# Second mixer: the delta branch woven into eight weight chunks, with results kept in DRAM

## The chip, the core and the metric

The kernel runs on one core of one Trainium2 chip. The metric is the device time of one execution in microseconds (us); of several executions the median is taken. The engines are named as in the profile: PE multiplies matrices (PEld loads its weights), DVE is the vector engine, ACT the scalar engine, POOL is GpSimd, SP issues DMAs.

## The reference, cut to what matters

Three blocks run one after the other on 512 tokens of width 1024, all in float32. The change is in the mixer of the second block. Its input `h` is multiplied by one wide matrix whose columns feed three recurrent branches (a: gated delta rule, b and c: attention with a decay per channel), their output gates and three "shares":

```python
proj = x @ w_in
(a_q, a_k, a_v, a_beta, a_dt, a_g, b_q, b_k, b_v, b_lr, b_g,
 c_q, c_f, c_i, c_g, m_a, m_b, m_c) = split(proj)
aq, ak, av = split(silu(causal_short_conv(concat[a_q, a_k, a_v], gdn_conv)))
aq = l2_normalize(aq) * 128 ** -0.5;  ak = l2_normalize(ak)
g_a = -exp(a_log) * softplus(a_dt + dt_bias)
o_a = gated_rms_heads(gated_delta_rule(aq, ak, av, sigmoid(a_beta), g_a), a_g, gdn_norm)
o_b = gated_rms_heads(diag_decay_linear_attention(b_q, b_k, b_v, log_alpha), b_g, gla_norm)
o_c = gated_rms_heads(diag_decay_linear_attention(silu(c_q), k_c, c_i, log_f), c_g, hgrn_norm)
y = (sigmoid(m_a) * (o_a @ w_br_a) + sigmoid(m_b) * (o_b @ w_br_b)
     + sigmoid(m_c) * (o_c @ w_br_c)) @ w_out
h = layer_norm(2 ** 0.25 * h + y)
```

## The kernel before

**Projections.** A weight chunk is 512 columns (1024 x 512 values, 2 MB), loaded by SP in two halves of 1 MB into one ring (`load_ahead`), cut by DVE into a high and a low part (`split_piece`, L122 and L124), and multiplied by PE in three products for each pair of tiles (L150 to L152): 96 matmuls of 128x512 for a chunk. The plan of chunks (`plan_two`) fixes their order, and a chunk is loaded and split about one chunk ahead. The split of the first half of chunk c+1 waits until PE has used the first half of chunk c, that of the second half until chunk c is done. `project` runs chunks alone, with two groups of four PSUM banks. `project_along` runs them with a `Side`: a piece of other work whose four engine parts are written as generators, each `yield` ending a step. A table for each engine says how many steps must stand in the engine's program before each slot; on PE there are eight slots for a chunk, of 12 matmuls each, in the order of `PAIRED`, with a choice of banks. Each turn of ACT that empties a bank is such a place too, and so is each split on DVE. So the order on each engine is fixed when the program is built, and a step that waits holds up all that stands behind it on its engine.

**Stages.** `stage` is a block in which the engines meet only by semaphores, with a barrier of all engines behind it (L45, L49). The second mixer is a row of such stages:

- `delta_in`: chunks `aqkv` (three, with a convolution on DVE) and `beta_dt` (8 columns wide, two short rows).
- `unit_rows` (L1502): norms of q and k by matmuls with ones (L1533), a reciprocal and a root, the factors spread by matmuls (L1537). SP also writes the 23 zero tiles of `moe_entries` here (L1511), 12 MB, wanted only in the later mixture of experts.
- soft maximum, decay, columns, values: short stages with one or two engines at work.
- `delta_half`, twice (two heads each), three stages each: `delta_scores`, `delta_inverse` (a triangular inverse by seven levels, each with 8 and then 16 matmuls per pair of groups, L1640 and L1645/L1646, and eight DVE passes), `delta_solve` (forward substitution over four token tiles, L1658, L1663, L1691, then outputs L1669).
- `close` for the branch: `gdn_gates` projects the gate `ag` and the share `ma` (three chunks; DVE normalizes the branch output beside them), `transpose` turns it, `gdn_out` multiplies it by `w_br_a` and by the share.
- `gla_in` (chunks `bqk`, `bv` and `blr`, 16 columns), gate and decays, `channel_decay` (L1750), `close`.
- `hgrn_in` (chunks `cq`, `cf`, `ci`), `hgrn_bound` and others, `channel_decay`, `close`; then `mix_T` and `out2`.

`core.h` holds the mixer's input from start to end, since `out2` adds it; `core.x` holds u and v of the delta branch and later the sum of the branches.

Of the kernel before, what the change touches and what calls it, by code (L numbers as in the profile page):

```python
# [7 lines left out]

# [367 lines left out]
def project_along(nc, core, name, xT, runs, banks, side, kt=KD):  # L376
# [6 lines left out]
    with stage(nc, name, "freed", "loaded", *side.signals) as (block, freed, *sems):  # L383
# [45 lines left out]
        @block.scalar  # L429
        def _(act):  # L430
            pace = Pace(side.act, act, sems)
            for i, (c, j, (_, _, _, how)) in enumerate(chunks):
# [1069 lines left out]
def unit_rows(nc, core, d, qkT):  # L1502

    n = 2 * GDN_HEADS
    with buffers(nc, squares=[P, n, SEQ], pick=[P, n, n], scale_row=[n, SEQ]) as (squares, pick, scale_row), \
            stage(nc, "unit", "picks", "squared", "summed", "inverted", "rooted", "spread") as (
                block, picks, squared, summed, inverted, rooted, spread):
        @block.sync
        def _(sp):
            for s in range(ROW_TILES):  # L1510
                sp.dma_start(core.moe_entries[s * P:(s + 1) * P, :], d["const_zero_rows"]).then_inc(core.entries_cleared, 16)  # L1511

        @block.gpsimd
        def _(pool):
            nc.gpsimd.memset(pick[:], 0.0)
            pool.drain()
            for f in range(n):
                done = nc.gpsimd.memset(pick[:, f, f:f + 1], 1.0)
            done.then_inc(picks, 1)

        @block.scalar
        def _(act):
            for f in range(n):
                nc.scalar.activation(squares[:, f, :], qkT[:, f, :], ACT.Square).then_inc(squared, 1)
            act.wait_ge(inverted, 1)
            nc.scalar.activation(scale_row[:], scale_row[:], ACT.Sqrt).then_inc(rooted, 1)

        @block.tensor
        def _(pe):
            pe.wait_ge(picks, 1)  # L1530
            for f in range(n):
                pe.wait_ge(squared, f + 1)
                mm = nc.tensor.matmul(core.ps[0:n, 0, :], pick[:, f, :], squares[:, f, :], start=f == 0, stop=f == n - 1)  # L1533
            mm.then_inc(summed, 1)
            pe.wait_ge(rooted, 1)
            for f in range(n):
                nc.tensor.matmul(core.ps[:, (f + 1) % 8, :], core.ident[0:n, f:f + 1].to_broadcast([n, P]), scale_row[:],  # L1537
                                 start=True, stop=True).then_inc(spread, 1)

        @block.vector  # L1540
        def _(dve):
            dve.wait_ge(summed, 1)
            nc.vector.tensor_scalar(scale_row[:], core.ps[0:n, 0, :], 1e-6, None, ALU.add)
            dve.drain()
            nc.vector.reciprocal(scale_row[:], scale_row[:]).then_inc(inverted, 1)
            for f in range(n):
                dve.wait_ge(spread, f + 1)
                nc.vector.scalar_tensor_tensor(qkT[:, f, :], qkT[:, f, :], GDN_DK ** -0.5 if f < GDN_HEADS else 1.0,
                                               core.ps[:, (f + 1) % 8, :], ALU.mult, ALU.mult)


def delta_half(nc, core, half, qkvT, cum_rows, cols, vb, u, o, masks):


    H = GDN_HEADS
    heads = (2 * half, 2 * half + 1)
    kind_beta, kind_cum, kind_minus = 0, 1, 2
    with buffers(nc, keys=[P, 2, PACKED], attn=[P, 2, PACKED], edge=[P, NT, P], diag=[P, 8, P], rhs=[P, 2, P]) as (
            keys, attn, edge, diag, rhs):
        inv, invT = (qkvT[:, q:q + 2, :].rearrange("p q (n t) -> p (q n) t", t=P) for q in (2 * H, 2 * H + 2))  # L1560
        part, prod = (core.tmp[:, q:q + 2, :].rearrange("p q (n t) -> p (q n) t", t=P) for q in (0, 2))
        with stage(nc, f"delta_scores{half}", "spread", "edged", "decayed", "scored", "applied") as (
                block, spread, edged, decayed, scored, applied):
            @block.tensor
            def _(pe):
                for n, h in enumerate(heads):
                    if n:
                        pe.wait_ge(decayed, n)
                    nc.tensor.matmul(core.ps[:, 0, :], core.ident[0:H, h:h + 1].to_broadcast([H, P]), cum_rows, start=True, stop=True).then_inc(spread, 1)
                    for m, first in enumerate((H + h, h)):  # L1570
                        for s in range(NT):
                            if n or m:
                                pe.wait_ge(applied, NT * (2 * n + m - 1) + s + 1)
                            nc.tensor.matmul(core.ps[:, 1 + s, 0:SEQ - s * P], qkvT[:, H + h, s * P:(s + 1) * P],
                                             qkvT[:, first, s * P:], start=True, stop=True).then_inc(scored, 1)

            @block.scalar
            def _(act):
                for n, h in enumerate(heads):
                    act.wait_ge(edged, n + 1)  # L1580
                    decay_strips(nc, core, 0, edge, lambda s: cols[:, kind_minus, h, s:s + 1], attn[:, n])
                    act.drain().then_inc(decayed, 1)

            @block.vector
            def _(dve):
                for n, h in enumerate(heads):
                    dve.wait_ge(spread, n + 1)
                    if n:
                        dve.wait_ge(decayed, n)
                    nc.vector.tensor_tensor(edge[:], core.ps[:, 0, :].rearrange("p (s t) -> p s t", s=NT),  # L1590
                                            core.causal[:].unsqueeze(1).to_broadcast([P, NT, P]), ALU.add).then_inc(edged, 1)
                    dve.wait_ge(decayed, n + 1)
                    for m, dst in enumerate((keys, attn)):
                        dve.drain()
                        for s in range(NT):
                            dve.wait_ge(scored, NT * (2 * n + m) + s + 1)
                            nc.vector.tensor_tensor(strip(dst[:, n, :], s), core.ps[:, 1 + s, 0:SEQ - s * P],
                                                    strip(attn[:, n, :], s), ALU.mult).then_inc(applied, 1)
# [50 lines left out]
        with stage(nc, f"delta_solve{half}", "gathered", "sided", "solved", "stored", "output", "copied") as (  # L1649
# [24 lines left out]
            def _(dve):  # L1674
                for t in range(NT):
                    if t:
                        dve.wait_ge(gathered, t)
# [1439 lines left out]
```

## Time and profile before

| | us |
|---|---|
| runs | 4644.2, 4658.12, 4653.43 |
| median | 4653.43 |
| profiled execution | 4639.73 |
| its span in the trace | 4637.9 |
| second mixer in it (2056.0 to 3079.4) | 1023.4 |

The profile is of one execution; stretches and durations come from it, and its own time is 13.7 us under the median of the runs. A stage begins and ends at a barrier; the stretches named here were cut at DVE's part of it. "Idle before" in a timeline is the time in which the engine did nothing ahead of an instruction, with the one that ended it. A matmul in full float32 is two records in the trace, a product of the split weights is one. The granted clock is given as a share of 2.4 GHz: 1.00 or 0.50 at any moment, in between as a mean.

### The profile page before, as it was taken

To read this page: it belongs to the slowest core of one execution; us is meant where nothing else is said; L and a number is where in the kernel's file an instruction comes from. 1 tells how busy PE (TensorE), PEld (TensorE's weight loads), DVE (VectorE), ACT (ScalarE), POOL (GpSimd) and SP (SyncE) were. 2 spreads that over 40 slices of the span, in tenths; PEclk is the share of its full clock that TensorE was granted. 3 is DMA by queue.
4 is the path that set the end of the run, shared out by engine and by line. 5 is a ranking of instruction groups with operands and counts; after the bars stand their busy time and mean duration, and the time that the engine had idled before them with its cause. 6 is when DMAs were issued, how large, how long until landed. Compare 5 with 4: busy or idle time off the path is not lost. (4 is left out here: it accounts for less than half of the span.)

```text
span 4637.9 us, 43415 instructions
## 1 busy us (share of the span) xinstructions
PE 3778.1 (81%) x15062; PEld 2573.6 (55%) x15062; DVE 2945.5 (64%) x5248; ACT 823.2 (18%) x1647; POOL 867.5 (19%) x777
## 2 busy tenths in 40 slices
PE   5999988778787777757787985966948897998987
PEld 3778764223232222234675975755736675776866
DVE  6554558878788787555553646546865557556774
ACT  1111011111111111012001205115731202311000
POOL 2010014344433444320000000014640000001001
PEclk8999989999999999978899998978979998998998
DMA  5423228999999999934012020118942122122322
GB/s 218 161 91 97 98 91 360 423 424 423 423 413 423 416 411 418 421 123 141 1 38 78 29 95 10 65 46 350 395 179 83 49 84 64 41 82 74 99 77 71
DMA packets 197011, 879.57 MB, mean 190 GB/s; under 512 B 21698, under 2 KB 23506, under 8 KB 118866
## 3 DMA queue, kind: packets, MB, share of 16 engines
q0 software_dynamic: 88624, 635.74, 33.4%
q1 hardware_dynamic: 107360, 238.56, 15.5%
q8 instruction: 113, 1.85, 0.2%
q10 hardware_dynamic: 820, 2.65, 0.1%
q14 instruction: 94, 0.77, 0.0%
HBM read 858.54 MB, written 30.41 MB: 192 GB/s over the span
## 5 line engine op out<-in xcount | busy, mean ns | idle before, releaser
L122 DVE CAST ring_high<-ring_raw 128x2048 fp32r<-128x2048 f32 (+3 forms) x186 | 212.3, 1141 | 712.1 <-PE psum L152 627.6
L1179 PE MATMUL psum<-slots_ring,evacuation_tmp 128*128 128x512 f32 x816 | 404.3, 618 | 103.0 <-DVE evacuation_tmp L1273 102.6
L150 PE MATMUL psum<-ring_high,h_features 128*128 128x512 f32 x1120 | 449.4, 401 | 25.3 <-DVE ring_low L124 13.0
L152 PE MATMUL psum<-ring_high,h_features 128*128 128x512 f32 x1120 | 441.9, 395 | 0.0
L151 PE MATMUL psum<-ring_low,h_features 128*128 128x512 f32 x1120 | 441.7, 394 | 0.0
L124 DVE TENSOR_TENSOR ring_low<-ring_raw,ring_high 128x2048 fp32r<-128x2048 f32 (+3 forms) x186 | 394.9, 2123 | 14.5 <-issue 0.4
L150 PE MATMUL psum<-h_features,ring_high 128*128 128x512 f32 (+4 forms) x920 | 365.5, 397 | 35.2 <-DVE ring_low L124 17.5
L554 POOL TENSOR_SCALAR mean_var<-mean_var 128x1 f32<-128x1 f32 (+3 forms) x45 | 12.9, 286 | 1957.1 <-DVEq L592 908.7
L1179 PE MATMUL psum<-slots_features,evacuation_tmp 128*128 128x512 f32 x612 | 302.1, 617 | 77.9 <-DVE evacuation_tmp L1273 77.8
L151 PE MATMUL psum<-h_features,ring_high 128*128 128x512 f32 (+4 forms) x920 | 363.6, 395 | 0.0
L152 PE MATMUL psum<-h_features,ring_low 128*128 128x512 f32 (+4 forms) x920 | 363.2, 395 | 0.0
L1179 PEld LDWEIGHTS psum<-slots_ring,evacuation_tmp 128*128 128x128 f32 x816 | 138.2, 189 | 368.2 <-DVE evacuation_tmp L1273 269.2
L1305 DVE CUSTOM_DVE_ANT_0 slots_ring<-slots_ring,h_tokens 128x1024 f32<-128x1024 f32 x204 | 249.8, 1224 | 100.7 <-DMA slots_ring<-in_peer_uv,expert 97.5
L1346 ACT ACTIVATE weight<-score 128x1 f32<-128x1 f32 x512 | 103.9, 203 | 1132.7 <-DVE score L1305 1132.5
L1126 POOL DMA_INDIRECT slots_ring<-in_peer_uv,expert x204 | 209.8, 1029 | 321.0 <-PE psum L1179 288.0
L150 PEld LDWEIGHTS psum<-ring_high,h_features 128*128 128x128 f32 x1120 | 214.0, 191 | 82.3 <-issue 31.5
L1179 PEld LDWEIGHTS psum<-slots_features,evacuation_tmp 128*128 128x128 f32 x612 | 104.0, 189 | 275.0 <-DVE evacuation_tmp L1273 199.9
L1179 PE MATMUL psum<-slots_mod,evacuation_tmp 128*128 128x512 f32 x416 | 206.7, 621 | 57.5 <-DVE evacuation_tmp L1273 57.4
L152 PEld LDWEIGHTS psum<-ring_high,h_features 128*128 128x128 f32 x1120 | 213.6, 191 | 46.0
L151 PEld LDWEIGHTS psum<-ring_low,h_features 128*128 128x128 f32 x1120 | 214.1, 191 | 43.8 <-issue 0.5
L1305 DVE CUSTOM_DVE_ANT_0 slots_features<-slots_features,h_tokens 128x1024 f32<-128x1024 f32 x153 | 187.4, 1225 | 73.2 <-DMA slots_features<-in_peer_uv,expert 70.4
L150 PEld LDWEIGHTS psum<-h_features,ring_high 128*128 128x128 f32 (+4 forms) x920 | 169.5, 184 | 83.3 <-issue 28.6
(545 smaller groups left out, 7017.5 us busy)
## 6 DMA issues: line engine op xcount, KB each, us to landing
ring_raw<-in_w_in SPq DMA_DIRECT2D x94, 1024.0 KB, 5.2
ring_raw<-in_w_up_pairs SPq DMA_DIRECT2D x20, 1024.0 KB, 5.0
ada_ring<-in_w_ada POOLq DMA_DIRECT2D x16, 1024.0 KB, 5.4
ring_raw<-in_w_out SPq DMA_DIRECT2D x12, 1024.0 KB, 5.1
moe_entries<-in_const_zero_rows SPq DMA_DIRECT2D x23, 512.0 KB, 16.3
row_room<-moe_entries SPq DMA_DIRECT2D x23, 512.0 KB
moe_results<-rows_out SPq DMA_DIRECT2D x23, 512.0 KB, 9.1
ring_raw<-in_w_down SPq DMA_DIRECT2D x10, 1024.0 KB, 4.8
```

The lines of the kernel that those rows point to most:

```text
L122: nc.vector.tensor_copy(high, whole)
L124: return nc.vector.tensor_tensor(low, whole, high.bitcast(F32), ALU.subtract)
L150: nc.tensor.matmul(out, a[0], b[0], start=start, stop=False)
L151: nc.tensor.matmul(out, a[0], b[1], start=False, stop=False)
L152: return nc.tensor.matmul(out, a[1], b[0], start=False, stop=stop)
L554: nc.gpsimd.tensor_scalar(v, v, eps, None, ALU.add).then_inc(done, 1)
L1126: nc.gpsimd.indirect_dma_start(out=slots[slot_of[n]], out_offset=None, in_=rows, in_offset=bass.IndirectOffsetOnAxis(ap=expert[:, t, i:i + ...
L1179: mm = nc.tensor.matmul(banks(t)[q], diagonal[:, n % DIAGONALS, :], slots[slot_of[n]][:, D + q * BANK:D + (q + 1) * BANK], start=i == 0, s ...
L1305: nc.vector.tensor_tensor_reduce(out=u, in0=u, in1=core.h[:, t, :], scale=1.0, scalar=0.0, op0=ALU.mult, op1=ALU.add, accum_out=score[:, i ...
L1346: nc.scalar.activation(weight[:, i:i + 1], score[:, i:i + 1], ACT.Gelu).then_inc(activated, 1)
```

## The change

**Order of the chunks.** The mixer's plan becomes: `aqkv` x3, `few` (24 columns: `beta_dt` and `blr` together), `ag`, `ma` x2, `bqk`, `bv`, `cf`, `cq`, `ci`, `bg`, `cg`, `br_a` x2, `mb` x2, `br_b` x2, `mc` x2, `br_c` x2, `out2` x2.

**Delta branch.** The twelve stages from `unit_rows` to the second `delta_solve` become one `Side`, `delta_scan`, with 90 steps on PE, 18 on ACT and 116 on DVE; `project_along` weaves it into the eight chunks from `ag` to `ci`. The chain keeps PSUM banks 0 to 5, the chunks use banks 6 and 7. The last level of each inverse leaves out the half that nobody reads (8 of 24 matmuls, and two DVE passes), and identities are copied by two instructions and not by sixteen. The zero tiles are issued by POOL, one for each level update of the inverse.

**Stashes.** Six of the eight chunks, and later `bg` and `cg`, are "stashed": ACT copies the bank to a row buffer, waits for its own copy, issues a DMA of 256 KB to DRAM from its own queue, and only then frees the bank. `ma` goes to `core.h`, whose contents were written to DRAM (`kept_h`, by POOL during `delta_in`) and are read back by SP at the start of `out2`. The stashes are read back as whole 1 MB tensors: gates by SP at the start of their stage, the inputs of branches b and c by POOL during the stage before.

**Closing a branch.** `close` becomes one `project_along` stage with `branch_features`: the norm, the gate, the transposes and the share's sigmoid go beside two chunks (`bg` and `cg`, then `mb`, then `mc`). `gla_in` and `hgrn_in` are gone; `hgrn_bound` applies the Silu to `q` in four ACT instructions.

```diff
@@ project_along: a turn of ACT
                     act.wait_ge(core.products, QUARTERS * c + t + 1)
-                    nc.scalar.activation(how[2](t, j), bank(NT * i + t), how[1]).then_inc(freed, 1)
+                    if how[0] == "stash":
+                        if stashes >= NT:
+                            act.wait_ge(stashed[t], 16 * (stashes // NT))
+                        nc.scalar.copy(core.stage_rows[:, t, :], bank(NT * i + t)).then_inc(evacuated, 1)
+                        stashes += 1
+                        act.wait_ge(evacuated, stashes)
+                        act.dma_start(how[1][j][:, t, :], core.stage_rows[:, t, :]).then_inc(stashed[t], 16)
+                        act.sem_inc(freed, 1)
+                    else:
+                        nc.scalar.activation(how[2](t, j), bank(NT * i + t), how[1]).then_inc(freed, 1)
             pace.rest()
+            for n in range(NT if stashing else 0):
+                act.wait_ge(stashed[n], 16 * (stashes // NT))
@@ delta_scan (its tables; PE of an inverse; POOL)
+DELTA_ORDER = {"pe": [0, 0, 1, 1, 2, 2, 3, 3, 4, 4, 6, 7, 8, 8, 9, 9, 10, 10, 12, 15, 19, 23, 25, 27, 29, 31, 35, 37, 39, 40, 41, 41,
...
+            for level in range(LEVELS):
+                turn = 2 * (LEVELS * half + level)
+                for g in range(2):
+                    pe.wait_ge(on.masked, turn + g + 1)
...
+                    for n in range(NT):
+                        mm = nc.tensor.matmul(bank(0, g)[:, n, :], of(part, g)[:, n, :], of(inv, g)[:, n, :], start=True, stop=True)
+                    mm.then_inc(on.first, 1)
+                    yield
+                for g in range(2):
+                    pe.wait_ge(on.scaled, turn + g + 1)
+                    for n in range(NT):
+                        if level + 1 < LEVELS:
+                            nc.tensor.matmul(bank(1, g)[:, n, :], of(invT, g)[:, n, :], of(prod, g)[:, n, :], start=True, stop=True)
+                        mm = nc.tensor.matmul(bank(2, g)[:, n, :], of(prod, g)[:, n, :], of(invT, g)[:, n, :], start=True, stop=True)
+                    mm.then_inc(on.second, 1)
+                    yield
...
+        for s in range(ROW_TILES):
+            pool.wait_ge(on.updated, s + 1)
+            pool.dma_start(core.moe_entries[s * P:(s + 1) * P, :], d["const_zero_rows"]).then_inc(core.entries_cleared, 16)
@@ delta_branch
+                    loads=[...], aside=keep_tokens(nc, core, d))
+            project_along(nc, core, "delta", core.hT, [stash("ag"), ("ma", 2, "token", ("act", ACT.Copy, columns(core.h))), stash("bqk"), stash("bv"),
+                                                       stash("cf"), stash("cq"), stash("ci")], (6, 7), delta_scan(...))
@@ branch_features (ACT and POOL; DVE's steps are those of gated_heads)
+BRANCH_FEATURES = {"pe": [0, 0, 0, 0, 0, 0, 2, 3, 3, 4, 4, 4, 4, 4, 4, 4], "dve": [4, 5, 9], "act": [1, 1, 3, 4, 6, 6, 6, 6]}
+        act.wait_ge(loaded, 16 * len(loads))
+        for t in range(NT):
+            nc.scalar.activation(gate[:, t, :], gate[:, t, :], ACT.Silu).then_inc(squashed, 1)
+        yield
...
+        inverse_root(nc, core, pool, mv[:, :, 1:2], 1e-6, var_ready, root_ready)
+        for dst, src in ahead:
+            pool.dma_start(dst, src).then_inc(come, 16)
@@ hgrn_bound
+                dve.wait_ge(keyed, 2 * H)
                 nc.vector.tensor_scalar(q[:], q[:], 128 ** -0.5, None, ALU.mult)
...
+                for h in range(H):
+                    nc.scalar.activation(q[:, h, :], q[:, h, :], ACT.Silu).then_inc(keyed, 1)
@@ second_mixer
-        project(nc, core, "out2", two_parts(yT), [("out2", 2, "token", ("axpy", ALPHA, columns(core.h)))])
+        project(nc, core, "out2", two_parts(yT), [("out2", 2, "token", ("axpy", ALPHA, columns(core.h)))], loads=[(core.h[:], core.kept_h)])
```

**PE at the start of the delta branch.** Before, with `L45` marking the barriers (L1533: sums of squares, L1537: factors spread, L1439 and L1731: transposes):

```order
L1533 MATMUL psum<-squares,pick 8x512 x8
L1537 MATMUL psum<-scale_row,ident 128x512 x8
L45 UNCONDITIONAL_BRANCH
L1435 UNCONDITIONAL_BRANCH
L1439 MATMUL psum<-ident,beta_row 128x4 x4
L1439 MATMUL psum<-ident,g_row 128x4 x4
L45 UNCONDITIONAL_BRANCH
L1727 UNCONDITIONAL_BRANCH
L1731 MATMUL psum<-ident,qkvT 128x128 x16
```

After, the last products of a slot (L151 to L153 there), the sums of squares (L1546), and the next slot:

```order
L151 MATMUL psum<-ring_high,h_features 128x512
L152 MATMUL psum<-ring_low,h_features 128x512
L153 MATMUL psum<-ring_high,h_features 128x512
L1546 MATMUL psum<-squares_13168,pick_13170 8x512 x8
L151 MATMUL psum<-ring_high,h_features 128x512
L152 MATMUL psum<-ring_low,h_features 128x512
```

Between each two groups of the chain there now stand 12 or 24 products (one or two slots); in the inverse up to four steps, which is a whole level, stand between two slots.

**ACT at the same place.** Before (L1524 squares, L1526 root, L1407 to L1413 soft maximum, L1716 and L1717 rates):

```order
L1524 ACTIVATE squares<-qkvT 128x512 x8
L1526 ACT_TABLE_LOAD
L1526 ACTIVATE scale_row<-scale_row 8x512
L45 UNCONDITIONAL_BRANCH
L1403 UNCONDITIONAL_BRANCH
L1407 ACTIVATE g_tmp<-g_row 4x512
L1410 ACT_TABLE_LOAD
L1410 ACTIVATE g_tmp<-g_tmp 4x512
L1413 ACT_TABLE_LOAD
L1413 ACTIVATE g_tmp<-g_tmp 4x512
```

After (L443 the copy of a bank, L446 the stash's DMA):

```order
L1658 ACTIVATE squares_13168<-qkvT 128x512 x8
L1661 ACT_TABLE_LOAD
L1661 ACTIVATE scale_row_13169<-scale_row_13169 8x512
L443 COPY stage_rows_12331<-psum 128x512
L446 DMA stash_ag<-stage_rows_12331 128x512
L1664 ACTIVATE g_tmp<-g_row 4x512
L1666 ACT_TABLE_LOAD
L1666 ACTIVATE g_tmp<-g_tmp 4x512
L1668 ACT_TABLE_LOAD
L1668 ACTIVATE g_tmp<-g_tmp 4x512
L443 COPY stage_rows_12331<-psum 128x512
L446 DMA stash_ag<-stage_rows_12331 128x512
```

The copies and DMAs that free PE's two banks now stand behind ACT's steps of the chain, and the next steps behind them.

## Rows read from the trace of the kernel before

**Rows 1.** Windows: stretch, length, busy PE, PEld, DVE, ACT, POOL; clock, DMA share, GB/s.

```profile
2056.00:3079.40 1023.40, 841.51 (x4444) 697.63 (x4444) 534.06 (x975) 184.58 (x359) 16.00 (x21) 0.90 0.18 58
2146.20:2376.50 230.30, 169.95 (x960) 133.64 (x960) 115.61 (x233) 30.14 (x60) 0.48 (x9) 0.80 0.18 58
2376.50:2452.30 75.80, 69.35 (x304) 56.81 (x304) 34.67 (x74) 11.81 (x18) 3.22 (x2) 0.98 0.20 64
2476.40:2528.20 51.80, 49.40 (x216) 38.25 (x216) 14.92 (x12) 5.38 (x9) 0.00 (x0) 1.00 0.27 83
2726.60:2795.70 69.10, 67.53 (x288) 55.42 (x288) 21.11 (x12) 8.47 (x13) 0.00 (x0) 0.97 0.31 98
```

**Rows 2.** Windows of three woven stages of the third block (the first two: 192 products).

```profile
3605.40:3702.10 96.70, 95.40 (x432) 69.23 (x432) 47.30 (x108) 23.66 (x64) 0.00 (x0) 0.95 0.12 37
3931.80:4047.40 115.60, 114.28 (x576) 86.95 (x576) 61.27 (x104) 42.52 (x120) 0.00 (x0) 0.94 0.12 37
3702.10:3750.90 48.80, 47.43 (x224) 39.27 (x224) 36.11 (x92) 14.07 (x21) 6.76 (x4) 1.00 0.29 98
```

**Rows 3.** Timeline, two products, 48 apart: start, length, engine, instruction.

```profile
2072.57 0.39 PE L150 MATMUL psum<-h_features,ring_high 128*128 128x512 f32 x1
...
2083.45 0.39 PE L150 MATMUL psum<-h_features,ring_high 128*128 128x512 f32 x1
```

**Rows 4.** Timeline: the passes of float32 matmuls of 512 columns, at full clock.

```profile
2153.51 0.09 PEld L1533 LDWEIGHTS psum<-squares,pick 128*8 128x8 f32 x1 [0.34 <-issue]
2153.94 0.09 PEld L1533 LDWEIGHTS psum<-squares,pick 128*8 128x8 f32 x1 [0.34 <-issue]
```

**Rows 5.** Timeline: PE in the inverse (first two), and the last solve.

```profile
2219.63 0.39 PE L1646 MATMUL psum<-qkvT,evacuation_tmp 128*128 128x128 f32 x2
2219.85 0.39 PE L1645 MATMUL psum<-evacuation_tmp,qkvT 128*128 128x128 f32 x2
...
2364.34 1.22 PE L1663 MATMUL psum<-rhs,qkvT 128*128 128x128 f32 x4 [0.70 <-DVE rhs L1681]
...
2375.62 0.59 ACT L1695 COPY o<-psum 128x512 f32<-128x512 f32 x1 [1.65 <-PE psum L1669]
```

**Rows 6.** PE by shape in the first woven stage, and all of its waits.

```profile
L2567 PE MATMUL psum<-v,weights 128*128 128x129 f32 x160 | 19.9, 279 | 0.0
...
PE psum L2557 <- PEq L49: 0.9, 1, 0.9
```

**Rows 7.** Timeline: the end of `delta_in` and what follows.

```profile
2141.77 1.23 DVE L122 CAST ring_high<-ring_raw 128x2048 fp32r<-128x2048 f32 x1 [0.20 <-issue]
2143.07 2.29 DVE L124 TENSOR_TENSOR ring_low<-ring_raw,ring_high 128x2048 fp32r<-128x2048 f32 x1
...
2147.39 1.01 PE L1533 MATMUL psum<-squares,pick 128*8 128x512 f32 x1 [7.82 <-ACT squares L1524]
```

**Rows 8.** Timeline: a DMA issued by ACT at the kernel's start.

```profile
4.27 0.49 ACTq L671 DMA_DIRECT2D mod<-in_b_ada  x1
```

**Rows 9.** DMA issues: tensors, queue, count, KB each, median us to landing.

```profile
ring_raw<-in_w_down SPq DMA_DIRECT2D x1, 256.0 KB, 3.3
x_tokens<-in_x SPq DMA_DIRECT2D x1, 2048.0 KB, 8.0
```

**Rows 10.** Window of `unit_rows` (columns as above); landing of all weight loads (L93).

```profile
2146.20:2175.90 29.70, 22.67 (x32) 6.44 (x32) 9.52 (x10) 6.17 (x10) 0.48 (x9) 0.67 1.02 339
...
DMA to landing us min/median/max: 1.8/5.1/15.8
```

**Rows 11.** DMAs issued by POOL in the first mixer: issue ns, min, median, most.

```profile
L718 POOL DMA_DIRECT2D ada_ring<-in_w_ada x16: 527/527/1040, 68.1 to 158.9; - x16
```

**Rows 12.** Timeline: ACT and DVE at the end of `hgrn_bound`.

```profile
2800.02 1.28 ACT L2061 ACT_TABLE_LOAD   x1
...
2801.32 2.19 ACT L2061 ACTIVATE k<-logs 128x512 f32<-128x512 f32 x4
...
2805.13 1.22 DVE L2051 TENSOR_SCALAR q<-q 128x2048 f32<-128x2048 f32 x1
```

More of the change, by code:

```diff
@@ L9 @@
+from collections import namedtuple
 from contextlib import ExitStack, contextmanager
@@ L382, in project_along @@
     bank = lambda n: core.ps[:, banks[n % len(banks)], :]
-    with stage(nc, name, "freed", "loaded", *side.signals) as (block, freed, *sems):
+    stashing = any(run[3][0] == "stash" for run in runs)
+    with stage(nc, name, "freed", *[f"stashed{n}" for n in range(NT if stashing else 0)], "evacuated", "loaded", *side.signals) as (block, freed, *sems):
+        stashed, evacuated, sems = sems[0:NT if stashing else 0], sems[NT if stashing else 0], sems[(NT if stashing else 0) + 1:]
         @block.sync
@@ L1499 @@
 LEVELS = 7
[L1502 to L1543, printed above, removed]
-            dve.drain()
[L1545 to L1549, printed above, removed]
@@ L1700, in delta_branch, with keep_tokens, pool_part, dve_part @@
+def keep_tokens(nc, core, d):
+    def pool_part(pool, kept):
+        pool.dma_start(core.kept_h, core.h[:]).then_inc(kept, 16)
+        pool.wait_ge(kept, 16)
+    def dve_part(dve, kept):
+        yield
+    return ("kept",), pool_part, dve_part
+STASHED = ("ag", "bqk", "bv", "cf", "cq", "ci", "bg", "cg")
+def delta_branch(nc, core, d, lr, o):
     H = GDN_HEADS
@@ L1712, in delta_branch @@
-        soft_maximum(nc, "delta_soft", [(g_row[:], g_tmp[:], 1.0, dt_bias[:], 0.0, 0.0)])
-        with stage(nc, "delta_decay", "ready", "scanned") as (block, ready, scanned):
-            @block.scalar
-            def _(act):
-                nc.scalar.activation(a_rate[:], a_rate[:], ACT.Exp).then_inc(ready, 1)
-                nc.scalar.activation(beta_row[:], beta_row[:], ACT.Sigmoid)
-            @block.vector
-            def _(dve):
-                dve.wait_ge(ready, 1)
-                nc.vector.tensor_scalar(g_tmp[:], g_row[:], a_rate[:], -1.0, ALU.mult, ALU.mult)
-                dve.drain()
-                nc.vector.tensor_tensor_scan(g_row[:], core.one_row[0:H, :], g_tmp[:], 0.0, ALU.mult, ALU.add)
@@ L1742, in delta_branch @@
-        for half in range(2):
-            delta_half(nc, core, half, qkvT, g_row[:], cols, vb, u, o, masks)
+                           (masks[:], d["const_levels"])], aside=keep_tokens(nc, core, d))
+        with buffers(nc, keys=[P, 2, PACKED], attn=[P, 2, PACKED], edge=[P, NT, P], diag=[P, 8, P], rhs=[P, 2, P]) as (
+                keys, attn, edge, diag, rhs):
+            stash = lambda name: (name, 1, "token" if name in ("ag", "bv", "ci") else "feature", ("stash", [core.stash[name]]))
+            project_along(nc, core, "delta", core.hT, [stash("ag"), ("ma", 2, "token", ("act", ACT.Copy, columns(core.h))), stash("bqk"), stash("bv"),
+                                                       stash("cf"), stash("cq"), stash("ci")], (6, 7),
+                          delta_scan(nc, core, d, qkvT, beta_row, g_row, g_tmp, dt_bias, a_rate, cols, masks, u, vb, o, keys, attn, edge, diag, rhs))
@@ L2061, in _ @@
                     nc.scalar.activation(k[:, h, :], logs[:, h, :], ACT.Sigmoid, scale=-1.0).then_inc(keyed, 1)
+                for h in range(H):
+                    nc.scalar.activation(q[:, h, :], q[:, h, :], ACT.Silu).then_inc(keyed, 1)
         tmp = core.tmp
@@ L3028, in build @@
         core.entries_cleared = sem("entries_cleared")
+        core.kept_h = nc.dram_tensor("kept_h", (P, NT, D), F32, kind="Internal").ap()
+        core.stash = {name: nc.dram_tensor(f"stash_{name}", (P, NT, BANK), F32, kind="Internal").ap() for name in STASHED}
+        core.stage_rows = over(nc, core.row_a, "stage_rows", [P, NT, BANK])
         with stage(nc, "later_start", "zeroed") as (block, zeroed):
```

515 lines of the change are left out of this document (328 added, 187 removed).

## The prediction

> **What bounds the kernel now.** I read the windows by stage first. The change touches only the second mixer, 1023.4 us of the span [rows 1]. PE is busy 841.5 us of it: where weight chunks run alone it is nearly always busy (`hgrn_in` 67.5 of 69.1, the gate stage with its transposes 69.4 of 75.8), but in the delta branch, from `unit_rows` to the second solve, it is busy 170 of 230.3 us at a mean clock of 0.80, and DVE only 115.6 [rows 1]. So that stretch is bound by the handing over between PE, DVE and ACT and by its barriers, and the rest mostly by PE. Then I looked for woven stages that exist already: in the third block PE is busy 95.4 of 96.7 and 114.3 of 115.6 us [rows 2], and its only wait is the one behind the barrier, 0.9 us [rows 6]. The question is what the delta chain and eight chunks take together.
>
> **PE's work in the woven delta stage.** At full clock: a product takes (2083.45 - 2072.57) / 48 = 0.227 us [rows 3]; 8 x 96 of them are 174.3 us. A pass of a float32 matmul with 512 columns takes 0.43 us [rows 4]; `unit_rows` has 32 such passes, 13.8 us. A float32 matmul of 128x128 takes 0.22 us, 0.112 a pass [rows 5]. The two inverses have 672 passes, less 32 that the change leaves out: 640 x 0.112 = 71.7. Solves and outputs have 160 passes, 17.9. Spread rows and scores are, in each half, 2 x 512 + 4 x 1280 columns in two passes, 12288 x 0.43 / 512 = 10.3 us, so 20.6. The transposes are about 4. Together 302.3 us. DVE's 115.6 plus eight splits of two halves, 3.5 each [rows 7], is 172, so DVE does not become the bound; ACT's 30 plus 32 copies and 24 DMAs is under 70.
>
> **What comes on top.** The same working for the existing woven stages gives 192 x 0.227 + 160 x 0.112 [rows 6] + 80 longer passes of 28672 columns, 24.1, together 85.6 us against 96.7; and 43.6 + 35.8 + 22.4 = 101.8 against 115.6 [rows 2]. Their clocks of 0.95 and 0.94 explain 4.8 and 6.9 of that (the slow time is twice 5 or 6% of the stage, and half of it is lost). What stays is 6.3 and 6.9: barrier, end and stalls. The new stage is three times as long and its chain is finer (90 steps on PE). I bound this term by 6.6 once and 21 in proportion, and take 12, nearer to the lower end, because the two stages show nearly the same whatever their length, and because I followed the tables across each chunk's boundary: each split on DVE stands ahead of a step that PE asks for one slot (2.7 us) or more later, and a half's split takes 3.5. The clock costs 0 to 7, I take 2.5: PE comes in warm (below), where the two stages began in a slow stretch. The chain's end has no cover: after the last slot four PE steps remain. Before, from the solve of the third tile to the last copy it takes 2376.2 - 2364.3 = 11.9 us [rows 5], of which PE's 60 passes are 6.7, so 5.2 on top. **Woven stage: 302.3 + 12 + 2.5 + 5.2 = 322 us, bounds 314 to 341.** It takes the place of 230.3 [rows 1], so 91.7 are added, and eight chunks leave elsewhere.
>
> **Stashes.** A stashed turn of ACT is a copy of 0.59 us [rows 5], its own wait, and an issue of 0.37 to 0.49 [rows 8], some 1.1 us before the bank is free. With two banks PE has one slot of 2.7 us between the last product of a tile and the next use of its bank. So a turn on time costs nothing; one behind a chain step can cost, which is in the stall term.
>
> **The other stages, each against its own.**
> - `delta_in` gets 24 more products, 5.4 us. They hide: DVE ends at 2145.4 with the next split and PE has been idle 7.8 us when the next stage starts [rows 7]. Cost 0.5; without that cover 5.4. This also keeps PE warm up to the barrier. The 2 MB of `kept_h` go out beside it; only POOL waits for them.
> - The three gate stages with transposes, 75.8 each (the third 75.7) [rows 1], become two-chunk stages with features. The third block's twin takes 48.8 with 32 transposes where 16 stand here [rows 2], less 16 x 0.13: 47, bounds 46 to 50. DVE has more statistics here, but by its parts the second tile is normed at about 16 us and PE asks for it at 17. The first of them ends with a stash: an issue and a landing that nothing covers. The nearest row is a transfer of 256 KB the other way, 3.3 us [rows 9]; I take 3.5 in all, bounds 2 to 6. So 50.5 + 47 + 47 in place of 227.3: 82.8 saved.
> - `gla_in`, 51.8, and `hgrn_in`, 69.1 [rows 1], are gone: 120.9 saved. Their inputs come back through POOL within a stage of 47 us or more, 3 MB at most, hidden.
> - `hgrn_bound`: ACT's four sigmoids end at 2803.5; one more table load, 1.28, and four Silus like them, 2.19, end at 2807.0, so DVE's last pass starts 1.9 us later than 2805.1 [rows 12]. Cost 1.9, bounds 1 to 4. The Trainium skill's page "ScalarE: Activation LUTs", section "What ACT_TABLE_LOAD costs", adds a drain of about 1.38 us to each load; by it this term would be 3.3. Here the load at 2800.02 is followed by the activation at 2801.32, 1.30 later: the trace shows no such drain.
> - `out2`: 2 MB land in 8.0 us [rows 9] and DVE waits for them, but its next split has to wait for PE's first half of a chunk anyway, 48 x 0.227 = 10.9 us. Cost 0, without that cover up to 5.
>
> **Sum.** 82.8 + 120.9 - 91.7 - 0.5 - 1.9 = 109.6 us saved. The profiled execution has 4639.7, so 4530; the median of the runs is 13.7 above it, so **4544 us** by the median. With all terms at their better ends some 14 less, at their worse ends some 38 more; with run-to-run spread 4522 to 4592.
>
> **Rival 1: the weave hides little.** A step waits for DVE or ACT and the product slot behind it waits too, since PE takes its program in order. Then the stage is the chain without its eleven inner barriers, about 220, and the products, 174: 394, so 72 more: 4616. For it: up to four steps stand between two slots in the inverses, and the order is fixed. Against: PE was busy four fifths of the inverse already, and the existing woven stages show no wait at all [rows 6].
>
> **Rival 2: the zero tiles hurt.** 12 MB of writes used to go out while PE was idle; they filled the DMA engines (share 1.02, 339 GB/s in `unit_rows`) and a weight load took up to 15.8 us [rows 10]. Now they go out beside the inverses, issued by POOL, each issue holding POOL for 0.5 to 1.0 us [rows 11]. If four weight halves came 10 us late, it would be 40 more: 4584. Against: the pieces are asked for about a chunk ahead, and a chunk lasts 40 us here. The Trainium skill's page "SBUF — State Buffer", section "SBUF: two separate sides", speaks against the move: POOL writes descriptors through a port that it shares with DVE, and is locked out while DVE copies in a two-port mode, so that such DMAs starve. By that rule the zero tiles and the stashes read back would only come later, and nobody waits for them within tens of microseconds. I saw no row that shows it.
>
> **Rival 3, slower than before: the two banks make it serial.** Every turn that frees a bank stands behind ACT's waits for the chain, PE's next slot waits for the bank, and the next chain step, behind that slot, waits too. Then chain, products and turns add up: 230.3 + 174.3 + 32 x 1.1 = 440, and with the clock at the chain's present 0.80 [rows 1] the products take a fifth more: 475. That is 153 more than I forecast: 4697. It decides from 432 us for the stage on, which is 110 us of new PE waits, 3.4 us at each of the 32 turns. Against: most turns have no ACT step before them.
>
> **How the numbers follow.** Forecast 0.82, rival 1 0.08, rival 2 0.06, rival 3 0.04. Predicted 4544. The range 4522 to 4592 takes in the bounds and rival 2; it leaves out rivals 1 and 3 and a tail of the forecast. Within 0.3% of before (14 us, about what a measurement can tell from no change) lies only the strip between rivals 1 and 3, 0.02. Slower by more 0.04, faster 0.94.
>
> **What would show it.** The woven stage 314 to 341 us long with PE busy over 97% and a clock above 0.95; no PE wait for ACT's `stage_rows` copies over 3 us in a place; the three gate stages at 47 to 51; PE idle at most 12 us at the end of the woven stage. I am wrong if PE's waits inside it exceed 20 us (then by whom: ACT copies mean rival 3, the splits of DVE behind a DMA mean rival 2, the chain's own DVE steps rival 1), if float32 passes between products take longer than 0.112 us, or if a stage outside the mixer changes.

## The result

| | before | after |
|---|---|---|
| median, us | 4655.34 (4644.20 to 4658.12) | 4536.53 (4522.51 to 4537.73) |
| profiled execution | 4639.73 | 4522.51 |
| second mixer in it | 1023.4 | 908.4 |
| ratio of the medians | | 0.9741, 95% interval 0.9723 to 0.9759 |

Four executions of each on the same chip. Forecast were 4544 us and 109.6 us less; measured are 4536.5 us, 118.8 less by the medians and 117.2 by the two profiled executions.

These are windows of the changed kernel, cut at the barriers like [rows 1]: the whole mixer, the woven delta stage, the first gate stage, the output product behind it, the other two gate stages, and `hgrn_bound`. Columns: length, busy PE, PEld, DVE, ACT, POOL, granted clock, DMA share, GB/s.

```profile
2054.80:2963.20 908.40, 802.91 (x4412) 672.72 (x4412) 523.74 (x927) 196.72 (x379) 34.22 (x54) 0.94 0.27 89
2145.50:2459.40 313.90, 310.28 (x1696) 254.81 (x1696) 165.60 (x233) 48.83 (x92) 12.60 (x32) 0.98 0.36 116
2459.40:2509.20 49.80, 45.62 (x208) 37.57 (x208) 26.47 (x66) 15.40 (x22) 5.95 (x7) 1.00 0.48 169
2509.20:2536.30 27.10, 25.41 (x96) 19.99 (x96) 14.17 (x16) 0.00 (x0) 0.00 (x0) 0.88 0.37 115
2630.30:2679.00 48.70, 47.26 (x208) 38.74 (x208) 26.58 (x66) 11.69 (x18) 5.40 (x6) 0.96 0.41 151
2831.00:2878.10 47.10, 45.64 (x208) 37.56 (x208) 26.48 (x66) 11.69 (x18) 3.20 (x2) 1.00 0.24 80
2707.90:2720.50 12.60, 0.00 (x0) 0.00 (x0) 4.33 (x14) 10.01 (x15) 0.00 (x0) 0.50 0.01 0
```

Where PE was busy 170 of 230.3 us before, it is now busy 310.3 of 313.9, and its list of waits in that stage is short (columns: the wait and what ended it, us in total, times, longest). The first row is the barrier, the others stand at the very end, behind the last product.

```profile
PE psum L151 <- PEq L50: 1.6, 1, 1.6
PE psum L1624 <- ACT x_tokens L1682: 1.1, 1, 1.1
PE psum L1630 <- DVE rhs L1802: 0.7, 1, 0.7
PE psum L1638 <- ACT x_tokens L1682: 0.5, 1, 0.5
```

So in 310 us with eight chunks and 90 chain steps there is no wait for a bank, a weight or the chain until the last product is out. The stage is 11.6 us longer than the 302.3 of work counted in the prediction, and the largest single part of that is the clock. Windows from 18.5 us into the stage on, the first one inside the spread matmuls (L1553, the L1537 of before; contraction of 8 rows):

```profile
2164.00:2167.80 3.80, 3.80 (x11) 1.66 (x10) 2.06 (x3) 3.32 (x4) 0.00 (x0) 1.00 0.18 69
2167.80:2174.60 6.80, 6.80 (x15) 4.24 (x14) 1.37 (x2) 4.99 (x7) 0.00 (x0) 0.50 0.10 39
2174.60:2181.40 6.80, 6.80 (x24) 4.07 (x24) 3.60 (x3) 0.00 (x0) 0.00 (x0) 1.00 0.00 0
2181.40:2184.80 3.40, 3.40 (x10) 2.63 (x9) 3.25 (x6) 0.00 (x0) 0.00 (x0) 0.50 0.70 207
2184.80:2459.40 274.60, 271.40 (x1581) 231.99 (x1579) 147.39 (x216) 33.85 (x71) 11.29 (x23) 1.00 0.37 120
```

In the first four windows, 20.8 us, PE is busy without a gap, and yet the granted clock is at 1.2 GHz for 10.2 us of them. If all that PE did there runs at half speed, that costs half of it, an estimate of 5.1 us. After that it stays at 2.4 GHz to the end.

The place that lost most is the end of the first gate stage: the last stash of `cg`, and the output product behind the barrier.

```profile
2505.70 0.59 ACT L443 COPY stage_rows<-psum 128x512 f32<-128x512 f32 x1 [2.13 <-PE psum L153]
2506.32 0.33 ACTq L446 DMA_DIRECT2D stash_cg<-stage_rows  x1
...
2509.84 0.76 PE L151 MATMUL psum<-ring_high,oT 128*128 128x512 f32 x1 [4.18 <-DVEq L255]
```

Copy, issue and landing (2.3 us) and the barrier leave PE idle for 4.18 us, where the same place without a stash has 1.56 (`ma_last` below); the first matmuls behind it take 0.63 to 0.76 us where 0.39 is the full-clock duration, and `gdn_out` takes 27.1 us against 24.2 before.

### The profile page after: what moved, and what is told of

Same layout as the page of the kernel before. It is cut to its first block and busy times, and to the rows that moved or that the text cites. A ratio compares the mean times of both kernels' runs of the same rounds, so it can differ in the third digit from the quotient of the medians.

```text
span 4520.7 us, 43069 instructions
## 1 busy us (share of the span) xinstructions
PE 3737.4 (83%) x15030; PEld 2546.6 (56%) x15030; DVE 2936.1 (65%) x5200; ACT 835.7 (18%) x1667; POOL 885.1 (20%) x810
## 5 line engine op out<-in xcount | busy, mean ns | idle before, releaser
L151 PE MATMUL psum<-ring_high,h_features 128*128 128x512 f32 x1120 | 451.5, 403 | 19.8 <-PEq L50 12.1
L153 PE MATMUL psum<-ring_high,h_features 128*128 128x512 f32 x1120 | 441.5, 394 | 0.0
L151 PE MATMUL psum<-h_features,ring_high 128*128 128x512 f32 (+4 forms) x920 | 366.8, 399 | 26.8 <-DVE ring_low L125 17.0
L153 PE MATMUL psum<-h_features,ring_low 128*128 128x512 f32 (+4 forms) x920 | 362.5, 394 | 0.0
L151 PEld LDWEIGHTS psum<-ring_high,h_features 128*128 128x128 f32 x1120 | 213.7, 191 | 78.7 <-issue 34.7
L153 PEld LDWEIGHTS psum<-ring_high,h_features 128*128 128x128 f32 x1120 | 212.8, 190 | 45.9
L151 PEld LDWEIGHTS psum<-h_features,ring_high 128*128 128x128 f32 (+4 forms) x920 | 169.0, 184 | 74.0 <-issue 28.8
```

The lines of the kernel that those rows point to most:

```text
L151: nc.tensor.matmul(out, a[0], b[0], start=start, stop=False)
L153: return nc.tensor.matmul(out, a[1], b[0], start=False, stop=stop)
```

## The experiments

The theory under test: the woven stage goes at PE's pace, its gain is the overlap of chain and products, and the stashes, the two banks and the zero tiles cost next to nothing where they lie. Each kernel is the changed kernel with one edit; its stages are compared one by one with the windows above, since the totals also carry what the clock does in other blocks (last section). Every median stands beside that of the kernel before on the same chip, 4656.1 to 4656.6 us.

### The chain ahead of the chunks

```diff
-DELTA_ORDER = {"pe": [0, 0, 1, 1, ...], "dve": [3, 5, 12, ...], "act": [2, 3, 4, ...]}
+DELTA_ORDER = {'pe': [90] * 64, 'dve': [116] * 15, 'act': [18] * 32}
```

> The changed kernel with one thing undone: every step of the delta chain is issued ahead of the eight weight chunks, on all three engines, and the chunks follow in one piece. No barrier comes back, and nothing is left out of the computation. My theory (the gain of the delta stage is that the chain's waits lie under the chunks' products, and the stage now goes at TensorE's pace): the chain alone took 230.3 us between its barriers; without these and with the stash instead of the gates some 205 to 220, and the chunks alone need 8 x 16 x 8 products of 0.17 to 0.23 us, about 174 us. The stage goes from 313.9 to 380 to 400 us, the kernel to 4600 to 4620 us. The rival (the weave hides little, what was gained is the barriers and the gates' stages): the woven stage is near serial already, and the kernel moves by less than 20 us.

Measured: 4601.34 us, ratio 0.9881 (0.9864 to 0.9897). The stage takes 381.9 us, 68 more; the other stages of the mixer are within 2 us of those above. Windows of the chain alone, and of the chunks alone:

```profile
2147.50:2349.10 201.60, 163.91 (x927) 129.33 (x928) 114.66 (x203) 29.48 (x59) 12.63 (x32) 0.83 0.23 71
2349.10:2524.10 175.00, 174.44 (x771) 144.16 (x770) 52.77 (x30) 19.46 (x33) 0.00 (x0) 1.00 0.38 120
```

The theory holds, the rival falls (it is rival 1 of the prediction): issued one after the other, the same work needs 68 us more. (A chunk has 96 products, so the chunks alone are 8 x 96 x 0.227 us; the 8 x 16 x 8 in the expectation was a wrong count with the right total.) The chain alone loses 38 us to idle time and runs at a clock of 0.83; the stage's PE busy time is 338.3 against 310.3 us for the same matmuls. So of the 68 us some 28 are the clock and 40 the idle time, 5.2 of them the landing of the last stash, which has nothing over it here. From 230.3 us before to the 201.6 of this chain without a weave are 28.7 us, for eleven inner barriers, the 32 passes left out (3.6 us) and the smaller cuts of the change; they weren't separated.

The second row prices the two banks as well: 64 slots in a row, each turn of ACT with a copy and 24 of them with an issue, and PE is idle for 0.6 us in 175. A turn of about 1.1 us costs next to nothing even where no chain step gives it time.

### A bank that is freed late

```diff
                         act.dma_start(how[1][j][:, t, :], core.stage_rows[:, t, :]).then_inc(stashed[t], 16)
+                        act.wait_ge(stashed[t], 16 * ((stashes - 1) // NT + 1))
                         act.sem_inc(freed, 1)
```

> The changed kernel, with one wait added in each of the 40 stashing turns: ScalarE tells TensorE that a bank is free only after the stashed tile has landed in DRAM, not after its copy out of the bank. This prices the two banks of a woven chunk. The turn of a bank goes from about 1.1 us (copy and signals) to about 1.1 + 2.3 to 4.8 us of landing, against a slot of 2.7 us of the other bank's products. My theory (the turn has slack of over 1 us now, so the two banks cost nothing): each turn now stalls TensorE by 0.8 to 3 us, 30 to 90 us in all, and by the point of 3.4 us per turn that I named, the stage nears the serial one. The rival (the two banks make it nearly serial already): the whole landing of each turn is added, 90 to 190 us.

Measured: 4542.29 us, ratio 0.9759 (0.9743 to 0.9776). Delta stage 325.6, 11.7 more, first gate stage 51.2, 1.4 more. Both expectations were too high. (There are 32 stashing turns, 24 of them in the delta stage; the 40 in the expectation was a miscount.) The two longest of PE's waits in the stage:

```profile
PE psum L1625 <- ACT x_tokens L1683: 8.1, 3, 6.8
PE psum L151 <- ACTq L448: 1.7, 1, 1.7
```

The timeline of ACT and PE around the longest:

```profile
2458.55 0.58 ACT L443 COPY stage_rows<-psum 128x512 f32<-128x512 f32 x1 [5.70 <-DMA stash_ci<-stage_rows]
...
2461.72 0.38 ACT L1683 ACTIVATE x_tokens<-psum 128x256 f32<-128x256 f32 x1 [2.59 <-DMA stash_ci<-stage_rows]
2462.16 2.93 PE L1625 MATMUL psum<-x_tokens,keys 128*128 128x128 f32 x12 [6.76 <-ACT x_tokens L1683]
```

And a window that takes in the end of that wait:

```profile
2458.40:2465.20 6.80, 2.93 (x12) 2.63 (x12) 0.08 (x1) 0.97 (x2) 0.00 (x0) 0.51 0.10 39
```

Freeing 24 banks more than 2 us late costs one bank wait, of 1.7 us. Around the end of the longest wait, 6.8 us, the clock is at 1.2 GHz for about as long, which the changed kernel doesn't have there; that and the longer waits make up most of the 11.7 us of the stage. I had set the late turn against a slot of 2.7 us, but the chain's work lies between the slots: 302 us for 64 of them is 4.7 us each on the mean. Only the last turns hurt, and in another way: ACT is held by the landings, and the chain's own step stands behind it in ACT's program. So a long wait in ACT's program was paid by the chain's step behind it, and hardly by the bank.

### The zero tiles, elsewhere

```diff
@@ zero_burst: POOL, no wait for the inverse's updates
         for s in range(ROW_TILES):
-            pool.wait_ge(on.updated, s + 1)
             pool.dma_start(core.moe_entries[s * P:(s + 1) * P, :], d["const_zero_rows"]).then_inc(core.entries_cleared, 16)
@@ zero_sp: SP instead, ahead of the stage's weight loads
+                for s in range(ROW_TILES):
+                    sp.dma_start(core.moe_entries[s * P:(s + 1) * P, :], core.zero_rows).then_inc(core.entries_cleared, 16)
```

> The changed kernel, with the wait ahead of each of GpSimd's 23 writes of zeros taken away: all 23 are issued by GpSimd at the start of the stage, back to back, in a queue that holds no weights. My theory: the burst shares the rings with the weights for about 36 us and nothing on TensorE waits for it, 0 to 5 us more. The rival (the zero writes take bandwidth or ports that the stage needs): tens of us, and TensorE's waits for weights show in the first 50 us of the stage.

> The changed kernel, with the 23 writes of zeros (512 KB each, 12 MB) taken from GpSimd, which issues one after each of its updates, and given to SyncE at the start of the woven delta stage, ahead of the loads of the weights. My theory (the zero writes cost nothing where they lie now because each is spread behind an update and no weight waits for it): here they stand ahead of the weights in their queue and take about 36 us of all 16 rings at the 339 GB/s of [rows 10], so the chunks' first products wait 10 to 30 us for their weights, and the kernel takes 10 to 30 us more. If the weights are far enough ahead in their buffers, 0. The rival that the zero writes hurt wherever they lie says at least as much as for the same burst issued by GpSimd.

Measured: the burst by POOL 4536.88 us, ratio 0.9743 (0.9727 to 0.9759), stage 316.6; by SP 4545.39 us, ratio 0.9752 (0.9735 to 0.9769), stage 322.7. Windows of the first 50 us of the stage, by POOL, by SP, and of the changed kernel:

```profile
2145.70:2195.70 50.00, 49.58 (x176) 31.27 (x176) 24.25 (x26) 17.43 (x24) 12.42 (x32) 0.90 0.96 327
```

```profile
2145.60:2195.60 50.00, 48.13 (x176) 30.84 (x176) 19.06 (x19) 17.44 (x24) 1.31 (x9) 0.93 0.97 325
```

```profile
2145.50:2195.50 50.00, 49.58 (x176) 31.55 (x176) 25.21 (x27) 17.43 (x24) 1.31 (x9) 0.90 0.31 103
```

The writes go from DRAM to DRAM (`const_zero_rows` to `moe_entries`). Rival 2 falls: the DMA engines can be full with them (share 0.96, 327 GB/s against 103) while PE is busy exactly as long, 49.58 us, with the same 176 matmuls. All 12 MB at once cost 2.7 us in the stage, most of it one more fall of the clock for 3.4 us and a chain wait of 0.9, and nothing in the median. The queue matters more: ahead of the weights, the same bytes cost 8.8 us in the stage and 8.8 in the median, just under the 10 to 30 that I expected. How they arrive at PE is in VectorE's timeline of that kernel and in the list of PE's waits:

```profile
2182.86 1.21 DVE L1716 TENSOR_TENSOR_SCAN g_row<-one_row,g_tmp 4x512 f32<-4x512 f32 x1
2195.49 1.23 DVE L123 CAST ring_high<-ring_raw 128x2048 fp32r<-128x2048 f32 x1 [11.41 <-DMA ring_raw<-in_w_in]
```

```profile
PE psum L1578 <- DVEq L1729: 7.8, 1, 7.8
```

No product waited for the late half chunk, as I had expected them to. DVE did, 11.4 us, and the chain's DVE step behind it (L1729) came late for PE. It is the same pattern as with the late bank: the wait passes to whatever stands behind it in order.

In the changed kernel the 23 writes, issued by POOL while DVE copies and multiplies, landed 4.0 us after their issue on the median. [rows 10] has the landings of the weight loads before, median 5.1. By the Trainium skill's "SBUF — State Buffer", section "SBUF: two separate sides", such DMAs can starve, since GpSimd is kept from writing their descriptors while DVE copies in a two-port mode; this trace doesn't show it.

### The features behind the gate chunks

```diff
-BRANCH_FEATURES = {"pe": [0, 0, 0, 0, 0, 0, 2, 3, 3, 4, 4, 4, 4, 4, 4, 4], "dve": [4, 5, 9], "act": [1, 1, 3, 4, 6, 6, 6, 6]}
+BRANCH_FEATURES = {"pe": [0] * 16, "dve": [0, 0, 0], "act": [0] * 8}
```

> The changed kernel, with the branch features (normalisation, gate and transposes) issued behind the gate chunks instead of between their products, in all three gate stages. The same work. Theory: they lie under the chunks now, where a gate stage takes 47 to 50 us against 46.6 us of products; behind them, each stage gets longer by most of the 75.8 - 47 = 28 us that the three stages lost, as far as ScalarE and VectorE cannot start early by themselves: 17 to 25 us a stage, 50 to 75 in all, about 4590 to 4610 us. The rival (the three stages lost their time by the missing barriers and the order of the work is of no matter): under 15 us in all.

Measured: 4582.36 us, ratio 0.9840 (0.9823 to 0.9857), 46 more. The three gate stages:

```profile
2463.60:2527.70 64.10, 48.26 (x208) 38.83 (x208) 26.65 (x66) 15.71 (x22) 5.96 (x7) 0.88 0.36 132
2648.00:2711.60 63.60, 49.86 (x208) 39.96 (x208) 26.65 (x66) 11.88 (x18) 5.41 (x6) 0.86 0.32 116
2865.80:2925.40 59.60, 48.24 (x208) 38.82 (x208) 26.76 (x66) 11.89 (x18) 3.20 (x2) 0.89 0.19 63
```

They take 14.3, 14.9 and 12.5 us more, 41.7 together, and the output products behind the last two, which start at a lower clock now, 2.5 and 1.5. The rival (barriers alone) falls; my 50 to 75 was too high. Without that order the three stages would have saved 40 of their 82 us, by a chunk less in each and the barriers between their parts; the order of the steps is worth the other 42.

### Two small edits that the profile asked for

```diff
@@ ma_last: delta stage and first gate stage exchange two chunks
-            project_along(nc, core, "delta", core.hT, [stash("ag"), ("ma", 2, ...), stash("bqk"), ...
+            project_along(nc, core, "delta", core.hT, [stash("ag"), stash("bg"), stash("cg"), stash("bqk"), ...
-            close("gdn", "gdn_norm_2", "ag", [stash("bg"), stash("cg")], "br_a", True,
+            close("gdn", "gdn_norm_2", "ag", [share("ma")], "br_a", True,
@@ spread_fine: a step ends after each pair of spread matmuls, not after the fifth of the eight
-            if f == 4:
+            if f in (1, 3, 5):
@@ spread_fine: the table, one pair ahead of each slot
-DELTA_ORDER = {"pe": [0, 0, 1, 1, 2, 2, 3, 3, 4, 4, 6, ...
+DELTA_ORDER = {'pe': [0, 0, 1, 1, 2, 3, 4, 5, 6, 6, 8, ...
```

With the exchange, the share `ma` gets its sigmoid on its way out of the bank, so four passes of ACT among the features of that stage go as well (its busy time falls from 15.40 to 11.69 us). The spread matmuls are eight in all, five of them in the 5.4 us that the expectation names; their cutting moves the later steps of PE's table by two.

> The changed kernel once more, unchanged, as the measure for the three that share its chip: 4530 to 4540 us.

> The changed kernel, with two pieces exchanged: the chunk of 1,024 columns that is stashed as ma in the delta stage goes to the first gate stage as its last share, where its gate is applied out of the bank, and the two chunks stashed at the end of the first gate stage (512 columns each) go to the delta stage in its place. As many products as before. Theory: in the changed kernel TensorE is idle 4.2 us at the end of the first gate stage for the landing of the last stash, and the output product behind it starts at the lower clock (27.1 against 24.2 us). With no stash in that stage both go: the gate stage 49.8 to about 47, the output product 27.1 to about 24.2, some 5 us in all, 4528 to 4532. If the end of the stage waits for something else (the features, the barrier), 0 to 2 us.

> The changed kernel, with the eight spread products of each head pair (contraction of 8 rows, 5.4 us in a row) cut into pairs that stand between the products of a weight chunk. The same work. In the changed kernel the granted clock fell to half for 6.8 and for 3.4 us while TensorE was never idle, first during such a row of spreads. Theory A (products with few rows in a row count as a quiet engine, and the clock falls for that): cut up, the clock holds and the stage is shorter by up to 5.1 us. Theory B (the fall comes from the stage's start, the idle time at the barrier ahead of it): the clock falls all the same, at about 22 us into the stage, and the kernel moves by less than 1 us.

> The changed kernel with both edits of the last batch: the stashes out of the first gate stage, and the spread products cut into pairs between the products of the chunk. The same work. Theory: the two touch different places (one took 2.6 us from the first gate stage and 2.8 us from the output product behind it, the other 3.6 us from the woven stage), so their gains add to about 9 us: woven stage about 310, first gate stage 47, output product 24; 4520 to 4528 us. The rival (a fall of the clock that is taken away at one place comes back at a later one): the sum of the stages is the same as with one edit alone, about 4530.

| kernel | median, us | ratio, 95% interval | delta stage | gate stage | output |
|---|---|---|---|---|---|
| changed, again | 4536.56 | 0.9746 (0.9732 to 0.9759) | 313.9 | 49.8 | 26.9 |
| exchanged chunks | 4529.67 | 0.9718 (0.9701 to 0.9735) | 314.0 | 47.2 | 24.3 |
| spreads in pairs | 4525.82 | 0.9727 (0.9709 to 0.9745) | 310.3 | 49.8 | 25.7 |
| both | 4525.20 | 0.9719 (0.9705 to 0.9732) | 310.3 | 47.3 | 24.3 |

Windows of the gate stage and the output product with exchanged chunks, and PE's first matmul of the latter; then, with the spreads in pairs, the delta stage and the stretch in which the clock fell in the changed kernel.

```profile
2461.90:2509.10 47.20, 45.63 (x208) 37.57 (x208) 26.48 (x66) 11.69 (x18) 5.95 (x7) 1.00 0.39 134
2509.10:2533.40 24.30, 22.63 (x96) 17.94 (x96) 14.16 (x16) 0.00 (x0) 0.00 (x0) 1.00 0.41 128
```

```profile
2509.74 0.47 PE L151 MATMUL psum<-ring_high,oT 128*128 128x512 f32 x1 [1.56 <-DVEq L255]
```

```profile
2150.20:2460.50 310.30, 306.34 (x1696) 251.54 (x1696) 165.67 (x233) 48.82 (x92) 12.63 (x32) 1.00 0.36 117
2172.40:2189.50 17.10, 16.81 (x65) 10.14 (x64) 10.43 (x12) 6.31 (x9) 0.00 (x0) 1.00 0.29 92
```

With no stash in the gate stage its end and the slow start behind it go, 2.6 and 2.6 to 2.8 us, as expected: PE is idle 1.56 us ahead of the output product (the single line above) and not 4.18. With the spreads in pairs, which begin at the same 18.7 us into the stage, the clock doesn't fall once in the woven stage, as theory A said and theory B did not. The stage is 3.6 us shorter, not 5.1: either some 1.5 us is paid for the cutting or the 5.1 was too much; which of them was not found. Both together have both gains in their stages, 8.9 us, and the mixer takes 897.2 us, 11.2 less than 908.4; most of the rest is the second gate stage, where the clock stays at 1.00 too. The combined kernel has the lowest median; it is 11 us under that of the changed kernel, which ran on another chip where the kernel before had the same median. The intervals of the ratios overlap or touch, so that both edits together beat one alone is shown by the stages and not by the totals.

## Why the prediction was right, and where its sum was off

**Woven stage, forecast 322 (314 to 341), measured 313.9.** It was the largest term, it came out at the lower bound, and it is the one whose parts were mis-sized. The work on PE, 302.3 by the count of passes, stands: on top of it and of the clock's 5.1 us there are 6.5 us in all, barrier (1.6), waits at the end (2.3) and 2.6 that no row names. I had 12 for stalls, barrier and end, and 5.2 more for the tail. The two woven stages in [rows 2] had left 6.3 and 6.9; I went half way to scaling that with the stage's length, and added the tail, which it partly holds already. Over stages of 97, 116 and 314 us it hardly grew. The clock I put at 2.5, it was 5.1 by the estimate above, because I looked for idle time only ([rows 7]: PE comes in warm) and not at what PE does. The two errors, 10.7 too much and 2.6 too little, point opposite ways, so that the sum was nearer than its parts is in part luck.

**Gate stages, forecast 50.5 + 47 + 47, measured 49.8 + 48.7 + 47.1.** 1.1 us more in all. The second has a clock of 0.96, hence its 1.7. The stash's end was forecast as 3.5 us; it costs 2.6, the 4.18 us of idle time less the 1.56 that stay without a stash, and the stage without one takes 47.2.

**`gdn_out`, forecast unchanged, measured 27.1 against 24.2.** Missed: I priced the uncovered landing and not the slow start of the product behind it. Here the idle time at the stage's end was paid again in the next one, and `ma_last` took both away together.

**Smaller terms.** `delta_in` 90.7 against 90.2 (forecast 0.5 more). `hgrn_bound` 12.6 against 11.0, forecast 1.9 more; the 3.3 that the added drain would make is not there. `out2` 47.9 as before. `hgrn_out` came 1.5 shorter, which I had not forecast.

**The sum.** The mixer saved 115.0, forecast were 109.6: 8.1 more from the woven stage, 2.9 less from `gdn_out`, the rest small. Outside the mixer the two profiled executions differ by 2.2 us, though no work there was changed: the stage with the experts takes 305.9 and not 302.9 us, one woven stage of the third block 112.4 and not 115.6. The prediction had named a change outside the mixer as a sign of being wrong. These are such changes, 3 us each and in opposite directions; the second goes with the clock, which moves as much between executions of one kernel (last section), the first stays unexplained. The other signs hold: PE busy 99% of the woven stage at a clock of 0.98, no wait for a stashed bank, the gate stages at 47 to 50.

**The rivals.** None of them holds, and each was tried by a kernel of its own. Rival 1 gave 394 us for the stage without overlap, and that state, built on purpose, took 381.9. Rival 2's 40 us for the zero tiles are 0 to 3 where nothing queues behind them, and 9 in front of the weights. Rival 3's mechanism, turns of ACT that hold up the slots, did not appear; with the banks freed late it made one wait of 1.7 us, and the 6.8 us behind the last turns were paid by the chain's step, far from the 110 us that it needs. Two sums of the prediction were a little off, without touching these readings: at a mean clock of 0.80 the products of rival 3 take a quarter more and not a fifth, some 9 us more than its 475; and the worse ends of the terms add to some 43 us, not 38, once an uncovered `delta_in` is counted.

## What to carry to other kernels

This chain took 230 us for 128 us of PE's work (302.3 less the 174.3 of the chunks), and it could be laid into the slots of matmul work that is bound by PE. For such a stage, count PE's passes at full clock and add the clock and some 6 to 8 us for the stage as a whole, not a share of its length: 6.3, 6.9, 6.5 and, with the spreads in pairs, 8.0 came out of the four stages here. Order matters within each engine's program: in two experiments a late DMA (a weight, a stash) cost the products that it was meant for 0 and 1.7 us, and the step of the chain that stood behind the waiting instruction 7.8 and 6.8. Leave no transfer to land at the end of a stage: here its 2.6 us of idle time were paid once more, as a slow clock in the next.

## What the hardware did that I had not expected

- The clock fell to 1.2 GHz with PE busy without a gap. It did so, 21 to 24 us into the woven stage (in one trace just behind the group of five, in the others inside it), in all seven traces of a woven stage in which the eight spread matmuls (8 rows contracted, two records each) stood in groups of five and three; in the two with these in pairs between products of 128 rows it stayed at 2.4 GHz through the stage. What in the group does it (the few rows, the full float32) wasn't separated, nor was the shift of the later steps.
- Two executions of the same changed kernel differ by 13.1 us (4522.51 and 4535.65), on chips that may not be the same, and the clock in another block makes more than that: the same 432 matmuls in the same stage take 96.7 us in the one and 106.9 in the other.

```profile
3492.40:3589.10 96.70, 95.40 (x432) 69.20 (x432) 47.20 (x108) 23.67 (x64) 0.00 (x0) 0.95 0.12 36
```

```profile
3490.70:3597.60 106.90, 105.54 (x432) 79.33 (x432) 47.19 (x108) 23.66 (x64) 0.00 (x0) 0.85 0.11 33
```

A later woven stage of that block adds 6.4 (112.4 and 118.8), and 3.5 us come back elsewhere. On one chip, too, the five executions with exchanged chunks took 4518.1 us twice and 4529.7 to 4530.6 three times. So a change of a few microseconds is better read from its stages than from medians of five executions.

And 327 GB/s of DMA from DRAM to DRAM cost PE nothing in those 50 us: it was busy 49.58 us of them, with the same matmuls, at a DMA share of 0.96 and of 0.31 alike.
